# One operand copy moved to GpSimd's queue, and four steps reordered, in a hybrid decoder block

## The reference, cut to what matters

```python
u = rms_norm(h, norm_g)
q, f_logit, iv, g_hg, u_s, z_s, gate_hg, gate_s5 = split(u @ w_in)
o = rms_norm(hgrn2_mix(q, f_logit, iv, lb))          # 8 heads, chunks of 64
y_hg = (o * silu(g_hg)) @ w_o_hg
ys = gelu(s5_mix(u_s, ...))                          # 32 groups of 16 channels
glu_a, glu_b = split(ys @ w_glu + b_glu)
y_s5 = (glu_a * sigmoid(glu_b) * silu(z_s)) @ w_o_s5
merged = sigmoid(gate_hg) * y_hg + sigmoid(gate_s5) * y_s5
h = h + merged @ w_out
h = h + (p @ w_ple) * sigmoid(rms_norm(h, ple_norm_g) @ w_ple_gate)
return rms_norm(h, final_norm_g)
```

## Time and profile before

| | |
|---|---|
| median of 3 runs | 2151.14 us |
| the profiled execution | 2150.19 us |
| its span, first to last instruction | 2148.6 us |
| mean granted TensorE clock | 0.997 of full speed |
| VectorE busy | 72% of the span |
| ScalarE busy | 49% |
| GpSimd busy | 14% |
| read from and written to memory | 232.33 MB and 94.37 MB |

### The profile page before, as it was taken

One profiled execution on the slowest core, in us unless ns is written; L12 is line 12 of the kernel. 1 busy time (PEld: TensorE's weight loads), 2 busy tenths in 40 slices (PEclk: granted clock), 3 DMA queues, 4 the chain that ended last, 5 costly groups with the idle time before them and its releaser, 6 DMA issues.

```text
span 2148.6 us, 29076 instructions
## 1 busy us (share of the span) xinstructions
PE 2119.1 (99%) x10178; PEld 1740.0 (81%) x10178; DVE 1554.5 (72%) x3140; ACT 1042.7 (49%) x1585; POOL 293.0 (14%) x518
## 2 busy tenths in 40 slices
PE   9999999999999999999998999999999999999997
PEld 6788888888888888887886788878888888888886
DVE  7775657787777778788887888566667567666756
ACT  6511235455455555575555555633544454354344
POOL 0011145000000000102322332211002001100100
PEclk9999999999999999999999999999999999999999
DMA  6454389311011011445568555675338435634632
GB/s 218 101 182 128 122 267 211 136 59 53 25 54 54 29 54 44 112 134 175 174 189 296 168 168 155 190 232 180 113 118 261 151 117 191 221 108 134 220 118 79
DMA packets 179599, 308.41 MB, mean 144 GB/s; under 512 B 40401, under 2 KB 85217, under 8 KB 179489
## 3 DMA queue, kind: packets, MB, share of 16 engines
q1 hardware_dynamic: 136816, 195.91, 29.3%
q0 software_dynamic: 38448, 102.69, 15.2%
q10 hardware_dynamic: 4224, 8.39, 1.1%
HBM read 232.33 MB, written 94.37 MB: 152 GB/s over the span
## 4 chain that ended last, share of the span: by engine, by line
PE 92%; DVE 3%; DMA 2%; ACT 1%; issue 1%; SPq 0%; DVEq 0%; ACTq 0%
PE c_bank L390 23%; PE c_bank L391 23%; PE c_bank L392 23%; PE c_bank L1499 5%; PE c_bank L1501 5%; PE c_bank L1500 5%; PE c_bank L797 1%; PE c_bank L774 1%; PE c_bank L784 1%; PE c_bank L795 1%; DMA u_hi<-terms_scratch 1%; PE c_bank L1536 1%; PE c_bank L1539 1%; PE c_bank L1519 1%; DMA c_raw<-w_glu_in 0%
## 5 line engine op out<-in xcount | busy, mean ns | idle before, releaser
L390 PE MATMUL c_bank<-u_hi,c_w_both 128*128 128x512 f32 x576 | 231.9, 403 | 2.2 <-DVE u_lo L1175 0.9
L392 PE MATMUL c_bank<-u_hi,c_w_both 128*128 128x512 f32 x576 | 224.2, 389 | 0.0
L391 PE MATMUL c_bank<-u_lo,c_w_both 128*128 128x512 f32 x560 | 218.6, 390 | 0.0
L2305 ACT ACTIVATE c_w_both<-c_raw 128x1024 fp32r<-128x1024 f32 x91 | 96.6, 1061 | 168.4 <-PE c_bank L392 150.9
L1057 DVE STREAM_TRANSPOSE hg_ken<-hg_ke 32x128 f32<-32x128 f32 x512 | 154.8, 302 | 6.5
L390 PEld LDWEIGHTS c_bank<-u_hi,c_w_both 128*128 128x128 f32 x576 | 108.2, 188 | 33.0 <-issue 5.5
L390 PE MATMUL c_bank<-t_oa_hi,c_w_both 128*128 128x512 f32 (+1 forms) x344 | 132.2, 384 | 0.0
L392 PE MATMUL c_bank<-t_oa_hi,c_w_both 128*128 128x512 f32 (+1 forms) x344 | 132.1, 384 | 0.0
L391 PE MATMUL c_bank<-t_oa_lo,c_w_both 128*128 128x512 f32 (+1 forms) x344 | 132.1, 384 | 0.0
L392 PEld LDWEIGHTS c_bank<-u_hi,c_w_both 128*128 128x128 f32 x576 | 108.2, 188 | 23.0
L864 ACT ACTIVATE hg_S<-hg_G,hg_coef 128x128 f32<-128x128 f32 x120 | 47.5, 401 | 156.2 <-DVE hg_G L1082 110.3
(11 more groups left out here) (392 smaller groups left out, 5655.2 us busy)
## 6 DMA issues: line engine op xcount, KB each, us to landing
c_raw<-sums_scratch SPq DMA_DIRECT2D x80, 256.0 KB, 2.8
c_raw<-w_in_in SPq DMA_DIRECT2D x64, 256.0 KB, 4.2
gates_scratch<-s_stage POOLq DMA_DIRECT2D x64, 256.0 KB, 4.4
t_ein<-gates_scratch SPq DMA_DIRECT2D x64, 256.0 KB, 4.5
c_raw<-w_o_hg_in SPq DMA_DIRECT2D x32, 512.0 KB, 3.8
c_raw<-w_out_in SPq DMA_DIRECT2D x32, 512.0 KB, 3.4
c_raw<-w_ple_gate_in SPq DMA_DIRECT2D x32, 512.0 KB, 3.3
sums_scratch<-w_in_in POOLq DMA_DIRECT2D x60, 256.0 KB, 11.9
```

The source lines that it names most:

```text
L390: pe.matmul(out, w_hi, u_hi, start=first, stop=False)
L391: pe.matmul(out, w_hi, u_lo, start=False, stop=False)
L392: return pe.matmul(out, w_lo, u_hi, start=False, stop=last)
L2305: act.activation(w_hi[u % WS], raw[u % RS], ACT.Copy).then_inc(w_hi_done, 1)
```

## The change

Six edits:

- copy 2 (the operand of product 5 in unit 10) is loaded by GpSimd in unit 9, ahead of that unit's first two stores, and no longer by ScalarE; it counts on another semaphore (`sums_kept`)
- in unit 10 ScalarE rounds term 7 behind piece 4 and no longer behind piece 2
- in unit 10 VectorE splits term 7 behind `piece(u, 4)` and no longer ahead of `scans`
- in unit 2 VectorE takes `piece(u, 1)` ahead of `owners` and no longer behind `add_c11`
- in the tail GpSimd waits for the split of the fourth weight unit before it loads the first `o` operands
- the `o` operands of the first tile are rounded and split in the four units of `os5` and no longer in those of `glu`

```diff
@@ copy_in
-        slot, base = ((5, 0), (6, 0), (3, 16))[n]
+        if n == 2:
+            return self.sums_kept, 8 * self.SUM_DMAS + self.COPY_DMAS + 2 * 16
+        slot, base = ((5, 0), (6, 0))[n]
@@ GpSimd, units
+                if u == 9:
+                    quads.load_copy(pool, 2)
                 store(u, C11)
                 store(u, C12)
@@ ScalarE, units
                 operands(u, 2, 3)
-                if u == 10:
-                    quads.round_term(act, 7)
...
                 piece(u, 4)
+                if u == 10:
+                    quads.round_term(act, 7)
...
-                operands(u, 5)
@@ VectorE, units
                     powers()
                     piece(u, 0)
+                    piece(u, 1)
                     owners()
...
-                if u not in (0, 10):
+                if u not in (0, 2, 10):
                     piece(u, 1)
                 if u == 10:
                     piece(u, 2)
-                    quads.split_term(dve, 7)
                 if use:
                     scans()
...
                 piece(u, 4)
+                if u == 10:
+                    quads.split_term(dve, 7)
                 gated(u, C11)
@@ GpSimd, tail
+            pool.wait_ge(w_lo_done, w0 + 4)
             for n, (what, k) in enumerate(XPRO):
@@ x_splits
-                return [("o", 2 * i), ("o", 2 * i + 1)] if sec == "glu" else []
+                return [("o", 2 * i), ("o", 2 * i + 1)] if sec == "os5" else []
```

## The result

| | before | changed |
|---|---|---|
| median | 2151.11 us (20 runs, 2148.99 to 2154.62) | 2156.77 us (20 runs, 2153.58 to 2369.05) |
| ratio | | 1.0022 [1.0016, 1.0028], or +4.7 us [3.4, 6.0] |
| profiled execution, its span | 2150.19, 2148.6 | 2159.19, 2157.6 |

The changed kernel is slower by 0.22%, just above the 0.2% that I had called the bound, and the interval leaves out zero: my "no change that a measurement can tell" did not hold. The forecast was 2153.1 within 2147.5 to 2158.0: the time is in the range, 3.7 us above the forecast. One of its 20 times, 2369.05, was a disturbed run (mean granted clock 0.85) and is left out of the ratio; the other 19 end at 2159.19, which is the profiled one. So this profile shows the slowest of them, 2.4 us above the median.

A forecast was written before the change was run, and what follows sets the result against it. TensorE was taken as the bound, busy 2119.1 of 2148.6 us, so only its idle and slow-clock time could move. The terms -2.4 (unit 2), -3.0 (tail), +2.5 (order) and +4.9 (copy) gave +2.0: median 2153.1, range 2147.5 to 2158.

The forecast's parts named there:

- Unit 2: Unit 2, piece 1 split ahead of `owners`: TensorE's gap before the sixth product goes, net gain 2.4 us (bounds 1.5 and 2.6).
- The order in unit 10: Unit 10, term 7's later round and split: idling moves from the sixth product to the seventh, costing 2.5 us.
- Rival C: Faster: VectorE reaches unit 10's last split early enough, so the 8.3 + 1.8 us go too: 2135.6; chance 0.09.
- The copy on GpSimd's queue: Units 9 and 10: the copy takes DMA share from terms ScalarE waits for, costing 4.9 us (bounds 0 and 8).
- The tail: `glu`, `os5`, `ohg`: waits on the weight block and split operand go, `o` operands just fit: gain 3.0 us (0 to 3.1).
- A: Rival: queues do not starve the terms, the copy costs 0 to 2 us: 2148.2 to 2150.2; chance 0.22.
- B: Rival, slower: GpSimd's C11 store waits behind the copy, delaying unit 10's first snapshot, or `o` operands miss: 2156.3; chance 0.18.
- my own case: The forecast itself: span 2150.6, median 2153.1 us, no measurable change (within 0.2%, 2146.8 to 2155.4); chance 0.51.

The follow-up runs named there:

- e2: Kernel before with only the unit 2 edit, `piece(u, 1)` ahead of `owners`: 2148.77 us, ratio 0.9984.
- e3: Kernel before with only term 7's round (ScalarE) and split (VectorE) moved behind piece 4 in unit 10: 2154.31 us, ratio 1.0015.
- e1: Changed kernel with copy 2 issued by ScalarE from its own queue again, all else as changed: 2150.99 us, ratio 0.9993 to the kernel before.
- e5: Kernel before with the unit 2 edit and ScalarE's later round of term 7, VectorE's split in its old place: 2146.94 us, ratio 0.9980.
- e4: Kernel before with only the two tail edits: 2149.40 us, ratio 0.9988.
- e9: Kernel before plus unit 2 edit, ScalarE's later round, GpSimd's tail wait, `o` pairs one unit earlier than changed, term 7 issued ahead of copy 2: 2143.69 us.
- e6: Kernel before with GpSimd's tail wait and the `o` pairs in `glu`'s last unit and `os5`'s first three: 2149.34 us, ratio 0.9986.

## Why the prediction was right, and where it was not

**Unit 2**, forecast -2.4: the spans show -2.4, e2's runs -3.4 [-5.4, -1.5]. Right. The gap is gone, and what comes back before the seventh product is 0.26 us where I had 0.2.

**The order in unit 10**, forecast +2.5: e3 +3.2 [1.3, 5.2], e1's unit 10 +2.8 (one profile). Right, and for its reason: the split of term 7 stands behind `scans`, `turn_forward` and two pieces, and starts at 1178.09 in e1, whose unit begins 2.5 us sooner than before's; I had 1181.0 (ending 1183.3) for a unit beginning at 1155.6. The 8.3 us of idling reappear as 7.84 before the seventh product, with the half clock behind them. Rival C's premise, that VectorE has room, was wrong for the change's order (the prediction's "no idle on VectorE after 1165.4" passes over one pause of 1.66 us in the earlier trace rows, too little for C); e5 shows that it would have had room with the split in its old place.

**The copy on GpSimd's queue**, forecast +4.9: the medians of e1 and the changed kernel are 5.8 apart, their units 10 by 6.3. The mechanism was right step by step: the copy issued at 1145.94 (I had 1146.7), terms 5 and 6 at 1159.57 and 1166.53 (1160.5 and 1166), the snapshot at 1164.34 (1164.5), a wait of 4.71 before the third product (4), one of 10.66 before the seventh ("10 us or more"), the last split over at 1188.62 (1188.2), C11's store down at 1163.6 (1162), 0.7 us ahead of the snapshot that it could have held. But unit 10 begins 1.0 us sooner than before, and taken from its start the round of term 6 begins at 12.0 us where I had 10.4, against 5.2 in e1. These 6.8 us are what the seventh product starts later than in e1 (34.15 against 27.40 us behind the unit's first matmul); 0.4 comes back behind the gap. So the term was mis-sized by 1.4 us: 6.3 for 4.9. While the copy ran q10 moved 0.10 MB/us, where I had 0.12, and the copy was over at 1162.0 (its second part landed 15.2 us after 1146.75), where I had 1159.5. Both point the right way; how much each is worth was not measured.

**The tail**, forecast -3.0 with bounds of 0 and 3.1: this is the step that failed in the changed kernel. The waits in `glu` and `os5` went as worked out (the block's load took 4.0 us), but "it fits by about 1 us" did not hold. I had the last `o` split over at 1436.6 to 1437.2 in the old times, on loads of 6 us and with the drains at no cost; it was over at 1448.09, which is 1440.0 in the old times. The last pair's loads took 7.8 us (the pair's before it 6.0, as I had taken between 3.5 and the 9.6 of the late weight block) and the last drains waited 1.65 and 1.85 us for `t_ein`, so that TensorE waited 2.09 us and ran at half clock behind it (3.4 us, from 1449.0): -3.0, +2.3 for the wait and +1.7 for the clock make +1.0, beside +0.9 measured. That is the case which I had named where it doesn't fit ("TensorE waits 1 to 3 us"), but given to the bound and not to the sum. Over the five profiles the edit is worth -1.4, over e4's runs -2.6 [-4.5, -0.6].

**The sum.** Corrected: -2.4, -1.4 (the tail's mean), +2.8, +6.3 make +5.3, beside +5.7 between the medians and +4.7 [3.4, 6.0] by the ratio; forecast was +2.0. Two terms were mis-sized in the same direction, the tail by 1.6 and the copy by 1.4, and the order's by 0.3. The profiled execution shows +9.0, since it is a bad case of the tail (2.4 above the mean) and has 1.4 us of a wait that the change doesn't touch.

**Rivals.** A (no starving) is excluded: q10 had half its bytes. B's time came nearest, 2156.3 for 2156.8, but not by its mechanism: GpSimd was never blocked, and the C11 store was in time, if only by 0.7 us: it landed at 1164.6 in the old times, at B's own mark of 1164.5, but ScalarE, held by term 5, reached the snapshot later still. Its second half, `o` operands late "on top of my own case", is what the profile shows. The time fell outside my own case (within 0.2%): the chance of slower by over 0.2%, 0.20, was too small for a forecast whose bounds lay lopsided: of the copy's cost the upper half was open, and the tail's gain was taken at its top end.

## What to carry to other kernels

When a copy is moved to another queue to be early, ask whose bytes it overtakes: the engines were full (3.08 MB in 8 us), and 2 MB ahead of operands that another engine takes in order cost 6 us, though the queue that issued them had been idle. Put the operands that still need work (a round, a split) ahead of those that need none, on the queue and in the engine's order, as in e9. And a step that "fits by 1 us" on a landing time read elsewhere is missed in a part of the executions (a wait in three of five profiles); moving it one unit earlier (e6) cost nothing to be seen, and its profiles have the whole gain.

## What the runs showed of the hardware beyond what was expected

- Queues in contention had equal packets and not equal bytes: 422 and 416 packets, 1.66 and 0.83 MB in 8 us.
- The granted clock behind like gaps differs from one execution to another. Behind the wait of 10.66 us the changed kernel's stretch of 1188 to 1194 has a mean granted clock of 0.58 (1.2 GHz for most of it), and behind a wait of only 2.09 us that of 1448 to 1453 has 0.66; behind waits of 1.71 (e1) and 1.22 us (e4) at the same place it did not fall. Unit 10 of unchanged code took 29.94, 30.02, 30.13 and 32.59 us in four kernels (before, e4, e6, e2), with 6.8, 10.2, 6.8 and 10.2 us at a granted clock of 0.5. The two stretches, TensorE's busy time first and PEclk third from the end:

```profile
1188.00:1194.00 6.00, 5.28 (x16) 3.97 (x18) 2.42 (x4) 0.85 (x2) 0.57 (x1) 0.58 0.34 119
```

```profile
1448.00:1453.00 5.00, 5.00 (x17) 3.93 (x16) 2.95 (x5) 2.21 (x3) 1.79 (x2) 0.66 1.01 278
```
